# Gates of two prompt blocks by indirect adding DMAs, of two by one-hot matmuls, with all routing done first

## What is computed

```
s = jnp.einsum('thsc,hskc->thsk', q, keys).astype(jnp.float32)
top_s, top_i = lax.top_k(s, PEER_TOPK)
cand = top_s[:, :, 0, :, None] + top_s[:, :, 1, None, :]
best_s, best_c = lax.top_k(cand.reshape(PEER_BLOCK, PEER_HEADS, PEER_TOPK * PEER_TOPK), PEER_TOPK)
i1 = jnp.take_along_axis(top_i[:, :, 0], best_c // PEER_TOPK, axis=-1)
i2 = jnp.take_along_axis(top_i[:, :, 1], best_c % PEER_TOPK, axis=-1)
e = (i1 * N_KEYS + i2).reshape(PEER_BLOCK, PEER_HEADS * PEER_TOPK)
gate = jax.nn.softmax(best_s, axis=-1).reshape(PEER_BLOCK, PEER_HEADS * PEER_TOPK)
hid = jnp.einsum('td,tkd->tk', xb, jnp.take(u, e, axis=0)).astype(jnp.float32)
wgt = (gate * jax.nn.gelu(hid)).astype(xb.dtype)
return jnp.einsum('tk,tkd->td', wgt, jnp.take(v, e, axis=0))
```

## Time and profile before

| | us |
|---|---|
| median of three runs | 5285.92 |
| the profiled execution, its own time | 5289.66 |
| its span, first to last instruction | 5288.0 |
| PE busy in the span | 4440.8 (84%) |
| PE at `hidden` (6144 matmuls) | 1509.7 |
| PE at `experts` (6144 matmuls) | 1420.5 |
| PE at the one-hot gates (2048 matmuls) | 255.5 |
| DVE busy | 2720.9 (51%) |
| ACT busy | 1452.1 (27%) |
| POOL busy | 376.4 (7%) |

### The profile page before, as it was taken

One profiled execution on the slowest core, in us unless ns is written; L12 is line 12 of the kernel. 1 busy time (PEld: TensorE's weight loads), 2 busy tenths in 40 slices (PEclk: granted clock), 3 DMA queues, 4 the chain that ended last, 5 costly groups with the idle time before them and its releaser, 6 DMA issues.

```text
span 5288.0 us, 75206 instructions
## 1 busy us (share of the span) xinstructions
PE 4440.8 (84%) x26376; PEld 3730.7 (71%) x26376; DVE 2720.9 (51%) x6287; ACT 1452.1 (27%) x2076; POOL 376.4 (7%) x254
## 2 busy tenths in 40 slices
PE   7667678978989799999885765889789897999997
PEld 7556477867767588888684654868667685888876
DVE  3454308765867344445235533196758672444442
ACT  3322023322323233332133211233223232333321
POOL 3100030000000000000040001200000000000000
PEclk9777889989999899999897768999899998999998
DMA  3100133467464666666220001345564646666651
GB/s 96 33 1 0 34 115 124 144 160 186 137 174 128 189 214 213 214 214 206 61 72 17 1 3 40 119 129 161 156 174 138 171 137 192 214 214 214 214 179 61
DMA packets 474218, 693.54 MB, mean 131 GB/s; under 512 B 29536, under 2 KB 292352, under 8 KB 473088
## 3 DMA queue, kind: packets, MB, share of 16 engines
q1 hardware_dynamic: 286384, 481.40, 28.8%
q10 hardware_dynamic: 168784, 143.16, 9.9%
q0 software_dynamic: 18944, 67.77, 4.4%
HBM read 546.20 MB, written 145.96 MB: 131 GB/s over the span
## 4 chain that ended last, share of the span: by engine, by line
PE 61%; DVE 15%; issue 11%; ACTq 5%; ACT 2%; DVEq 2%; DMA 1%; POOL 1%; SPq 0%; POOLq 0%
PE ps L823 26%; PE ps L764 14%; PE ps L598 9%; ACTq L1048 5%; PE ps L789 3%; DVE m L1400 2%; PE ps L606 2%; PE ps L571 1%; DVE m L1427 1%; DVE m L1420 1%; DVE m L1415 1%; DVE m L1424 1%; DVE m L1526 1%; DVE m L1464 1%; DVE m L1466 1%
## 5 line engine op out<-in xcount | busy, mean ns | idle before, releaser
L764 PE MATMUL ps<-m,m 128*128 128x512 f32 x6144 | 1509.7, 404 | 239.1 <-ACT m L1045 211.6
L764 PEld LDWEIGHTS ps<-m,m 128*128 128x128 f32 x6144 | 1169.7, 193 | 523.3 <-ACT m L1045 228.0
L823 PE MATMUL ps<-m,m 128*128 128x512 f32 x6144 | 1420.5, 394 | 18.8 <-DVE m L1552 18.8
L823 PEld LDWEIGHTS ps<-m,m 128*128 128x128 f32 x6144 | 1157.5, 188 | 281.8 <-DVE m L1552 19.6
L1400 DVE TENSOR_TENSOR m<-m,m 128x1024 fp32r<-128x1024 f32 x512 | 624.2, 1221 | 809.5 <-ACT m L1038 798.7
L1038 ACT ACTIVATE m<-m 128x1024 fp32r<-128x1024 f32 x512 | 540.0, 1055 | 755.5 <-DMA m<-in_v 727.5
L1547 DVE TENSOR_TENSOR m<-m,m 128x512 f32<-128x512 f32 x256 | 177.1, 692 | 681.8 <-DMA m<-expert_inputs 681.5
L598 PE MATMUL ps<-m,m 128*128 128x272 f32 x3648 | 461.3, 289 | 53.1 <-POOL m L519 53.1
L598 PEld LDWEIGHTS ps<-m,m 128*128 128x128 f32 x3648 | 460.6, 190 | 54.6 <-issue 54.6
L1045 ACT ACTIVATE m<-ps 128x512 f32<-128x512 f32 x256 | 152.9, 597 | 1224.9 <-PE ps L764 952.5
L1526 DVE TENSOR_SCALAR m<-m,m 128x128 f32<-128x128 f32 x1024 | 352.3, 344 | 9.4 <-issue 9.4
(11 more groups left out here) (213 smaller groups left out, 3164.9 us busy)
## 6 DMA issues: line engine op xcount, KB each, us to landing
m<-in_ut SPq DMA_DIRECT2D x256, 512.0 KB, 3.8
m<-in_v SPq DMA_DIRECT2D x256, 512.0 KB, 3.7
expert_inputs<-m ACTq DMA_DIRECT2D x256, 256.0 KB, 3.9
gate_matrix<-m ACTq DMA_DIRECT2D x8, 8192.0 KB, 44.7
m<-gate_matrix SPq DMA_DIRECT2D x256, 256.0 KB, 3.8
m<-expert_inputs SPq DMA_DIRECT2D x256, 256.0 KB, 4.0
m<-in_w_in SPq DMA_DIRECT2D x44, 512.0 KB, 3.8
m<-in_wq SPq DMA_DIRECT2D x32, 512.0 KB, 4.0
```

The costliest lines, as they stand in the source:

```text
L764: last = mm(ps[:, 4 + j % 2, :], lhs[j][:, k, :], rhs[:, k, 0:SEQ], start=(k + w == 0), stop=(k == KD - 1 and w == 2))
L823: last = mm(ps[:, m, :], lhs[j][:, m, :], rhs[j], start=(first and n == 0), stop=(final and n == 2))
```

## The change

All five blocks are routed first, and each block's tiles need no gate work: DEC over 3 groups of four tiles, and each prompt block over 4 (`QUADS_N`). `route` no longer ends with the softmax; that is a function of its own (`soft`), called in the middle of the next block's `route` (`early`), so that ACT's exponential (`soften`) stands behind a whole block's tiles.

The gates of blocks 0 and 1 go into DRAM by indirect DMAs on POOL (`put`). The columns of these blocks in the gate matrix are zeroed in each layer by one DMA of 16 MB from a small zero buffer, issued by SP behind the loads of `w_in`. `put` then issues, for each of the 128 picks, one DMA of 128 floats (one for each token) that adds the gate to the cell that the pick names. Sixteen of them, one head's picks, are issued together; the next head waits until they have landed. That is 256 DMAs in a layer.

The gates of blocks 2 and 3 are still made by one-hot matmuls, behind the routing: block 2 over 4 groups (`hot`), then 2 groups without, then block 3 over 4 groups, then 3 groups to the end. `save` sends a block's 8 MB in eight DMAs of 1 MB, each behind one `gelu` of the groups that follow.

`hidden` rotates over four PSUM banks (4 to 7) instead of two, and over four buffers to DRAM. The rows of `u` and `v` for the sample tokens have four buffers each; the dots move to the end: the first eight to the last two groups of `hot(1)`, the other 24 two to a tile behind it. POOL fetches rows of `u` between and after the adds, and rows of `v` only when both saves have landed.

The core of the diff:

```diff
-QUADS_DEC, QUADS_A, QUADS_B = 2, 3, 4
+QUADS_DEC, QUADS_N = 3, 4
+PUT_B = 2
+HOT_B = NB - PUT_B
+HOT_Q = BLK // GT // 2 // RING
+HOT_0 = [QUADS_DEC + NB * QUADS_N, QUADS_DEC + NB * QUADS_N + HOT_Q + 2]
+QUADS_END = HOT_0[1] + HOT_Q
+PIECES = 8
-ROWS = 2
+ROWS = 4
...
+                sp_.dma_start(gate_d[:, :, 0:PUT_T], zeros.unsqueeze(1).to_broadcast([P, NK, PUT_T])).then_inc(gate_zero, 16)
                 sp_.wait_ge(lru_done, L + 1)
...
+                def put(b, q):
+                    if q > 0:
+                        pool.wait_ge(gate_put[b], L * (16 * SLOTS) + q * (16 * TOPK))
+                    else:
+                        pool.wait_ge(place_ready, L * PUT_B + b + 1)
+                    passed(pool)
+                    for k in range(q * TOPK, (q + 1) * TOPK):
+                        cell = place[b][:, k:k + 1].bitcast(U32)
+                        pool.indirect_dma_start(gate_cells, bass.IndirectOffsetOnAxis(ap=cell, axis=0), gate[b][:, k:k + 1], None,
+                                                compute_op=ALU.add).then_inc(gate_put[b], 16)
...
-                            last = mm(ps[:, 4 + j % 2, :], lhs[j][:, k, :], rhs[:, k, 0:SEQ],
+                            last = mm(ps[:, 4 + j, :], lhs[j][:, k, :], rhs[:, k, 0:SEQ],
...
+                turn(0)
+                hot(0)
+                with pe.Fori(HOT_0[0] + HOT_Q, HOT_0[1]) as g:
                     for j in range(RING):
-                        hidden(g + (NB * QUADS_N + QUADS_DEC), j)
+                        hidden(g, j)
+                turn(1)
+                hot(1)
+                with pe.Fori(QUADS_END, QUADS) as g:
+                    for j in range(RING):
+                        hidden(g, j)
...
+                def save(b, m):
+                    n = NK // PIECES
+                    with act.Fori(m, m + PIECES // RING) as g:
+                        for j in range(RING):
+                            gelu(g, j)
+                            piece = bass.ds(g * (RING * n) + (j - m * RING) * n, n)
+                            act.dma_start(gate_d[:, piece, (PUT_B + b) * BLK:(PUT_B + b + 1) * BLK], stage[:, piece, :]).then_inc(gate_saved, 16)
...
+                left = (QUADS - QUADS_END) * RING
+                for n in range(left):
+                    if n <= left - RING:
+                        ahead(QUADS_END + n // RING, n % RING)
+                    for i in (half + 2 * n, half + 2 * n + 1):
+                        if i < DOTS:
+                            dot(i)
```

More of the change, by code:

```diff
@@ L153, in trunk @@
         epst = take(2)
+        zeros = take(256)
         A0 = aligned(top[0])
@@ new lines, in _ @@
+                act.wait_ge(q_saved, L * 16 + 16)
+                scores(L * NBLK, DEC)
+                with act.Fori(0, QUADS_DEC) as g:
+                    for j in range(RING):
+                        gelu(g, j)
+                soften(0, DEC)
+                for b in range(NB):
+                    scores(L * NBLK + b + 1, BLK)
+                    with act.Fori(QUADS_DEC + b * QUADS_N, QUADS_DEC + (b + 1) * QUADS_N) as g:
+                        for j in range(RING):
+                            gelu(g, j)
+                    soften(b + 1, BLK)
@@ L1067, in gates @@
                     av(stage[:, :, bass.ds(g * (2 * RING * GT) + k * GT, GT)],
-                       ps[:, 6 + k % 2, :].rearrange("p (j n) -> p n j", j=GT), ACT.Copy).then_inc(gmat_out, 1)
-                def save(b, col):
-                    act.wait_ge(gmat_out, L * GROUPS + b * (BLK // GT) + BLK // GT + 2)
-                    act.dma_start(gate_d[:, :, col], stage[:, :, :]).then_inc(gate_saved, 16)
-                for j in range(RING - 1):
-                    high(0, j)
-                scores(L * NBLK, DEC, s2_dec)
@@ new lines, in load_hot @@
+                def load_hot(at):
+                    dve.drain()
+                    copy(selq, sel[:, :, at])
+                    dve.drain()
+                dve.wait_ge(selT_out, L * HOT_B + 1)
+                passed(dve)
+                with dve.Fori(0, HOT_Q) as g:
+                    load_hot(bass.ds(g * (2 * RING * GT), 2 * RING * GT))
+                    for j in range(RING):
+                        hots(0, g, 2 * j)
+                        hots(0, g, 2 * j + 1)
+                        ahead(g + HOT_0[0], j)
@@ new lines, in _ @@
+                with dve.Fori(HOT_0[0] + HOT_Q, HOT_0[1]) as g:
+                    for j in range(RING):
+                        ahead(g, j)
+                dve.wait_ge(selT_out, L * HOT_B + 2)
+                passed(dve)
+                half = HOT_Q // 2 * RING
+                for g in range(HOT_Q):
+                    load_hot(slice(g * (2 * RING * GT), (g + 1) * (2 * RING * GT)))
+                    for j in range(RING):
+                        hots(1, g, 2 * j)
+                        hots(1, g, 2 * j + 1)
+                        ahead(g + HOT_0[1], j)
+                        if g * RING + j >= half:
+                            dot(g * RING + j - half)
```

325 lines of the change are left out of this document (180 added, 145 removed).

## The result

The changed kernel takes 5021.12 us, median of four runs (5020.53 to 5023.67), against 5287.39 us for the kernel before (5283.55 to 5290.91): a ratio of 0.9497, 95% interval 0.9481 to 0.9514, so 266 us faster. The forecast was 4935 us, which against the same 5287.39 is 352 us faster (the prediction's 355 counts from the profiled execution). The sign and the range hold; 86 us of the gain, about 43 in each layer, did not come.

A forecast was written before the change was run, and what follows sets the result against it. PE in the hidden stage, about 1012 us a layer, with pauses mostly for ACT's gelu, was the bound. 5289.66 - 399 + 8 + 4 + 30 + 6 = 4939, forecast 4935 us; bounds 4883 to 5027 (0.66), range 4870 to 5150.

The forecast's parts named there:

- Gates of two blocks: In hidden, PE no longer makes gates for 64 tiles at 1.77 us each: -113 us.
- The big save: In hidden, PE's 211.6 us of gelu waits and slow matmuls behind long pauses go: -224 us.
- Waits at the end of the routing: PE's waits at the turn and for the sample block's low parts go, with slow tiles behind them: -62 us.
- Routing at 5.6 us a tile: While DVE routes, PE still waits for low parts: +8 us (0 to 30).
- Pieces of block 2: Block 2's save pieces share eight tiles with other transfers, ACT's wait for landing included: +4 us (0 to 20).
- The tail: At the end of hidden, block 3's pieces and row fetches ask too much: 15 us a layer, +30 us (0 to 70).
- The start of the experts: PE's first wait there grows because loads wait for pieces and dots, whose gelu moved later: +6 us (-4 to 20).
- The zeros: Zeroing 16 MB on SP's queue delays a load 30 us under the mixer's cover: nothing, or 30 us a layer uncovered.
- The adds: POOL's 256 adds a layer, at 1.6 us each like fetches, stay hidden ahead of the dots: 0 us.
- The rival with its limit of 1.95 us: Adds too slow: above 1.95 us each, dots wait on POOL and PE stops in the tail; slower overall, chance 0.14.
- adds a little late: Adds on POOL at 2.1 to 2.6 us each make the time fall between 5027 and 5275 us; chance 0.05.
- The other way into that rival: DVE's work beside POOL slows it to 3 us an add, at the same price; 0.03 of the 0.14.

The follow-up runs named there:

- more_between: The changed kernel with tiles served at 14 places of the routing instead of 10: 5024.74 us.
- spread: The changed kernel with gates finished in their own block, 14 service places in routing, first v loads issued earlier, and dots spread over the one-hot stretches: 4889.38 us.
- early_v: The changed kernel with SP's first four v loads of the expert stage issued ahead of its waits for adds, pieces and dots: 5005.98 us.

## Why the prediction was right and where it was not

*Gates of two blocks* (-113): right. PE's gate line falls from 127.7 to 65.9 us in layer 1, -124 for both.

*The big save* (-224): the waits for the gelu are gone, all 211.6. But the term credits pieces and banks together, and the runs separate them. Two of four saves in a layer went with the one-hot work of two blocks: without pieces and banks four pauses of 24 us (96.1 in all) are left of eight. The pieces took those; the banks nothing that can be told.

*Waits at the end of the routing* (-62): the turn's 13.0 us a layer are gone. Those for `low` are not, which leads to the first wrong step.

*Routing at 5.6 us a tile* (+8, 0 to 30): some 50 for both layers by more_between (25 us earlier at the first gates), above the upper end. The step that failed is "A routing of some 60 us holds ten calls of `between`, where PE wants 10.7 tiles". The routing takes about 71 us (from 869 to 940), in which PE at 5.6 us wants 12.7 tiles, and ten calls don't feed it.

*Pieces of block 2* (+4): about right. Eight tiles beside them take 44.84 us, as in the earlier trace rows without them; ACT then waits 7.25 us for the save to land, and PE stands 0.62, 0.61 and 0.82 us at the first tables behind it, some 4 us for both layers.

*The tail* (+30, 0 to 70): too dear. PE waits 3.8 us in it in layer 1. The engines moved 346 GB/s over the tail's 71.7 us, not the 269 to 318 of the earlier trace rows.

*The start of the experts* (+6, -4 to 20): 20.9 and 20.4 us in the two layers, +41, outside its bounds. I named that the loads wait for pieces and dots and that the dots' gelu stands behind the last tile, and priced both at 3 us. Part of what did not fit into the tail is paid here: spread, which moves rows out of the tail, shortens this wait. The sum of tail and start, some 49, was not far from the 36 that I had for them: the work was seen, its place was not.

*The zeros* (0): right, the first scores come at 792.09 against 791.37.

*The adds* (0, at 1.6 us each all in): the largest miss, 27.3 and 28.8 us of wait at the tables. The price was taken from a fetch: 1.34 us from start to start. It is 1.84, and 2.16 all in, because accumulating costs POOL 0.58 us more than storing (1.54 against 0.96 in the usual instruction). The rival with its limit of 1.95 us names what happened ("adds a little late", 0.05), and its formula is near: the dot stood at 736 us after the first scores, not 700, and the adds started at 208, so the limit was (736 - 208) / 256 = 2.06 us. The adds took 552 us where 528 were free; these 24 us and the row's 4.6 are the wait at the dot.

Per layer the additions that I had put at 24 (routing 4, pieces 2, tail 15, start 3) came to 68.5 (18.7 of waits for `low` beyond the 3.5 that were there, 28.9 at the tables, 20.9 at the start): 44.5 more. The terms that save came out about 1 us better than forecast in layer 1, which leaves the 43. That the time lies within the stated 4883 to 5027 is partly luck: the additions of both layers, 137 us, nearly fill the 140 of all high ends together, but 58 of them, at the tables, belong to a term that stands in that sum with nothing.

The other way into that rival, POOL slowed by DVE's work beside it, is settled by two windows of POOL's adds, the first with DVE busy 40.19 of 55 us, the second with DVE standing:

```profile
1005.00:1060.00 55.00, 51.41 (x214) 40.82 (x213) 40.19 (x80) 16.50 (x20) 44.91 (x27) 0.97 0.61 121
1528.00:1550.00 22.00, 4.73 (x21) 3.48 (x19) 0.00 (x0) 1.54 (x2) 18.38 (x12) 0.67 0.36 48
```

44.91 / 27 = 1.66 and 18.38 / 12 = 1.53 us: at most 0.13 us of an add can be DVE's. The lock of which the Trainium skill warns ("SBUF — State Buffer", section "SBUF: two separate sides") is not what sets the price here. The Trainium skill's fixed 2.0 us for a DMA from GpSimd ("DMA: Bandwidth & Descriptors", section "Anatomy of one DMA — SWDGE (gpsimd) path") would have given, by the prediction's estimate, a wait of 12 us a layer, the right side of the limit; but the trace has a wait for the landing only at the ends of heads, 2.1 to 5.6 us each in layer 1, and between adds the 1.54 us of POOL itself.

Of the signs: waits for the gelu under 60 us and no issue on ACT above 10 held; the stage without the wait at its end, which is what the 1012 counts, fell to 859 (792.09 to 1651.14) and not to 835; the adds are 1.84 us apart and not 1.3, and ended 24 us behind the need, not 90 ahead.

## What to carry to other kernels

A slow queue costs nothing by itself; it costs what stands behind it, so look up which later item it delays, and either start the queue earlier (53 us here) or put that item between its entries (spread). When two waits lie one after the other on one path and the second ends at a fixed time, taking away the first shows nothing (5024.74 against 5021.12) until the second is gone. Gathered rows belong where the DMA engines have room (a busy share of 0.62 in the one-hot stretches, 0.94 in the tail with the start of the experts): the same 32 fetches, most of them moved out of a stretch with 8 MB of saves, took another 9 us off the start of the next stage (17.30 to 8.75).

## What the runs showed of the hardware

An indirect DMA that adds 128 cells of 4 bytes costs POOL 1.54 us, one that stores them 0.96, one that gathers 128 rows of 4 KB 0.94. An add makes 144 packets, a store 32: the software queue has 18944 packets in the kernel before, 92672 in the changed kernel and 35328 with stores, so the 512 adds brought 73728 and the 512 stores 16384. Fewer packets and less POOL time went with a program 315 us slower, with PE and DVE standing between single instructions; that is shown twice and not explained. The engines moved 383 GB/s over 60 us (early_v, 1600 to 1660), where the two stretches of the earlier trace rows had 318 and 269.
